# The dt step of a float32r decoder layer: its products cut at other column widths, h_hi and h_lo in one tile

## The chip, the cores and the metric

The kernel runs on one core of a Trainium2 chip. The metric is the device time of one execution in microseconds, lower is better; it is given as the median of three runs. All times below are microseconds unless a unit stands beside them, and times of day in the trace count from the start of the profiled span.

## The reference

One inference step of a decoder layer with two SwiGLU feed-forward blocks and a mixer between them, for 256 prompt tokens and 8 sample tokens (264 columns in all), D_MODEL 2048. The mixer begins with one large product, and the last 16 columns of that product are the `dt` values:

```python
proj = h @ p['w_in']                      # (tokens, 2048) @ (2048, IN_COLS)
xl, gl, z, xbc, dt_raw = jnp.split(proj, [o1, o2, o3, o4], axis=-1)
...
dt = jax.nn.softplus(dt_raw.astype(jnp.float32) + p['ssd_dt_bias'].astype(jnp.float32))
A = -jnp.exp(p['ssd_A_log'].astype(jnp.float32))
y, ssm_hT = ssd_scan(xs4, dt, A, ...)     # the state space scan uses dt as step width
```

The change concerns how `h @ w_in` is made for the `dt` columns, nothing else.

## The kernel before

Activations are held transposed: features on the 128 partitions, the 264 tokens (256 of the prompt, `NT`, and 8 samples, `NB`; together `COLS`) in the free dimension. A weight matrix is therefore the stationary operand, 128 x 128 at a time, and the activations stream past it, 264 columns a product, into a PSUM bank of 512 columns.

Every product is made three times in float32r: the weight w is split into `w_hi` (rounded to float32r) and `w_lo` (the rest), the activation h into `h_hi` and `h_lo`, and the product is w_hi h_hi + w_hi h_lo + w_lo h_hi. All three add up in the same PSUM columns.

The weights come in 90 steps of 8 pieces. For each piece SyncE issues the transfer into `raw` (four slots, two pieces in each; the slot is filled again when VectorE has split both pieces of the step before), ACT rounds it into `w_hi` (line 686, after the transfer and after TensorE has used the piece four places before it), VectorE makes `w_lo` = raw - w_hi (line 1007), and TensorE multiplies (lines 1660 to 1662, in `piece`). ACT and VectorE run up to four pieces ahead of TensorE. In each quarter j of a step ACT's and VectorE's queues hold first the splitting of pieces 2j+3 and 2j+4 (with j = 3 that is pieces 1 and 2 of the next step), then what else the step asks of them.

The steps around the change:

- step 38, xbc 0: a full step, 8 pieces of 4 x 256 weight columns, two 128-column halves each; 192 products.
- step 39, dt (`S_DT`): 8 pieces of 2 x 128 weight columns, one half; 48 products of 264 columns into bank 0 of `main`. At its end ACT copies `main[:, 0, 0:264]` to `dtq` in SBUF (line 824) and counts up `drained[0]`; it stands in ACT's queue behind the rounding of pieces 1 and 2 of step 40.
- step 40, xbc 1: a full step again. Its first pieces go to banks 0 and 1, so its first product waits until `drained[0]` shows that the dt result is copied. In VectorE's queue stand, in this order: w_lo of pieces 1 and 2 of step 40, the convolution of xbc 0 (`conv_taps(1)`, line 1214 on), w_lo of pieces 3 and 4.
- step 41, xbc 2: after its first pieces TensorE turns `dtq` round (line 1570 and 1574), and VectorE goes on with the softplus.

PSUM bank 1 of `main` (`main[:, 1, :]`) is not used by the dt step of the kernel before.

Of the kernel before, what the change touches and what calls it, by code (L numbers as in the profile page):

```python
# [22 lines left out]
F32R = mybir.dt.float32r  # L23
ALU = mybir.AluOpType
# [119 lines left out]
def build(nc, ins, outs):  # L144
    with ExitStack() as ctx:
# [5 lines left out]


        x = sb("x", [P, KD, COLS])
        h_hi = sb("h_hi", [P, KD, COLS], F32R)
        h_lo = sb("h_lo", [P, KD, COLS], F32R)
        raw = sb("raw", [P, 4, 2 * PIECE])
        w_hi = sb("w_hi", [P, 4, PIECE], F32R)
        w_lo = sb("w_lo", [P, 4, PIECE], F32R)
# [104 lines left out]
        aff_ready, hhi_ready, h_ready = sem("aff_ready"), sem("hhi_ready"), sem("h_ready")  # L263
        act_chain, dve_chain, pool_chain = sem("act_chain"), sem("dve_chain"), sem("pool_chain")

        dt_turned, cs_spread, dt_exp, dA_ready = sem("dt_turned"), sem("cs_spread"), sem("dt_exp"), sem("dA_ready")
        abs_ready, decl_sub, decl_ready, dexp_ready = sem("abs_ready"), sem("decl_sub"), sem("decl_ready"), sem("dexp_ready")
        samp_spread, samp_placed = sem("samp_spread"), sem("samp_placed")
# [730 lines left out]
        def _(dve):  # L999
# [298 lines left out]
            def dve_tasks(kind, t, j, s, o_, e_):  # L1298
                u = 4 * t + j
                if kind == "dt" and j == 3:  # L1300
                    conv_taps(1)
                if kind == "xbc":
                    if j in (1, 3) and u != 3:
# [261 lines left out]
        def _(pe):  # L1565
# [97 lines left out]
                last.then_inc(piece_used, 1)  # L1663


            def rows_batch(b):
                bank = (b5, b6)[b % 2]
                if b >= 2:
                    pe.wait_ge(rows_placed, b - 1)
                if b == 0:  # L1670
                    pe.wait_ge(consts_ready, 1)
                    pe.wait_ge(c_rows, C_ROWS)
                    for tile in range(C_TILES):
                        last = turn(bank[:, tile * P:(tile + 1) * P], rowbuf[:, tile, :])
                elif b == 1:
                    pe.wait_ge(early_rows, EARLY_ROWS)
                    for tile in range(C_TILES, E_TILES):
                        last = turn(bank[:, (tile - C_TILES) * P:(tile - C_TILES + 1) * P], rowbuf[:, tile, :])
                elif b < 2 + KD // 2:
                    pe.wait_ge(x_rows, 32)  # L1680
                    k = 2 * (b - 2)
                    for kk in range(2):
                        for c in range(2):
                            last = turn(bank[:, kk * NT + c * P:kk * NT + (c + 1) * P],
                                        xrows[:, c, (k + kk) * P:(k + kk + 1) * P])
                else:
                    pe.wait_ge(late_rows, LATE_ROWS)
                    pe.wait_ge(std_ready, 1)
                    at = E_TILES + 4 * (b - 2 - KD // 2)
                    for n, tile in enumerate(range(at, min(at + 4, ROW_TILES))):  # L1690
                        rows = min(P, ROWS - tile * P)
                        last = (turn if rows == P else turn_part)(
                            bank[:, n * P:n * P + rows], latebuf[0:rows, tile - E_TILES, :], *([rows] if rows < P else []))
                    if b == 3 + KD // 2:
                        last = MM(bank[:, 448:448 + 3 * NHEAD], ones[0:1, :], heads_row[0:1, :], start=True, stop=True)
                last.then_inc(rows_turned, 1)
# [131 lines left out]
            def pe_tasks(kind, t, j, e_):  # L1828
                u = 4 * t + j
                if kind == "xbc":  # L1830
                    if u == 4:
                        pe.wait_ge(drained[0], E_DT + 1)
                        pe.wait_ge(std_ready, 2)
                        turn(b6[:, 0:P], dtq[:, 0:P])
                        turn(b6[:, P:2 * P], dtq[:, P:2 * P])
                        turn_part(b6[0:NB, 2 * P:3 * P], dtq[:, 2 * P:2 * P + NB]).then_inc(dt_turned, 1)
                    if u == 7:
                        pe.wait_ge(dA_ready, 1)
                        both = dA[:, 0:2, :].rearrange("p c h -> p (c h)")
                        MM(b7[:, 0:32], tri[:, :], both, start=True, stop=True)  # L1840
                        MM(b7[:, 32:64], ones[:, :], both, start=True, stop=True).then_inc(cs_spread, 1)
                    if u == 10:
                        pe.wait_ge(dexp_ready, 1)
                        MM(b6[:, 0:2 * P].rearrange("p (a n) -> p a n", a=2), ones[0:NB, :],
                           sumsq[0:NB, :, 0:P], start=True, stop=True).then_inc(samp_spread, 1)
                if kind in ("lru", "z"):
                    r = u + (16 if kind == "z" else 0)
                    if r == 0:
                        prep(0)
                    if r == 2:  # L1850
                        states_turned()
                    if r == 3:
                        states(0)
                    if 5 <= r <= 12:
                        y_item(r - 5)
                    if 16 <= r <= 23:
                        y_item(r - 8)
                    if 4 <= r <= 11:
                        bcast(r - 4)
                    if r == 13:  # L1860
                        prep(1)
                    if r == 14:
                        states(1)
                    if 15 <= r <= 22:
                        bcast(r - 7)
                if kind == "lru":
                    if j < 2:
                        col_rows(2 * t + j)
                    else:
                        gates(2 * t + j - 2)  # L1870
                if kind == "out" and u == 1:
                    pe.wait_ge(captured, 10)
                    pe.wait_ge(h_captured, 4)
                    for tile in range(OUT_TILES):
                        bank = (b5, b6)[tile // 4]
                        if tile == 4:
                            pe.wait_ge(std_ready, 3)
                        last = turn(bank[:, (tile % 4) * P:(tile % 4 + 1) * P], outcol[:, tile * P:(tile + 1) * P])
                        if tile == 3 or tile == OUT_TILES - 1:
                            last.then_inc(out_turned, 1)  # L1880
                if kind == "out" and u == 15:
                    pe.wait_ge(out_rows_ready, 1)
                    sums_and_products(4, S_FF2)
# [14 lines left out]
            for n, seg in enumerate(plan):  # L1898
# [11 lines left out]
                for i, last in turns(seg):  # L1910
                    for k in range(per):
                        s, e_, o_, par = at_step(seg, i, k)
                        for j in range(4):
                            if j == 0 and s not in GAP_STEPS:
                                for a in products_at.get(s, ()):
                                    ada_product(a)
                            for m in (2 * j, 2 * j + 1):
                                if s == S_OUT and m == 2:
                                    pe.wait_ge(y_placed, 16)
                                    sumsq_total(3)  # L1920
                                if pk == "full":
                                    par_m, at = full_place(s, m)
                                else:
                                    par_m, at = par, sum(PIECES[pk][:m])
                                piece(s, m, pk, par_m, at, None if pk == "full" and par_m else h_base,
                                      act_base, (e_, o_)[par_m] if at == 0 else None, kind == "down")
                            if j == 2 and s in vec_ends:
                                ada_turn(vec_ends[s])
                            if kind not in ("up", "down"):
                                pe_tasks(kind, what or 0, j, e_)  # L1930
                            if j == 2 and S_LAST <= s < S_LAST + 4:
                                g = s - S_LAST
                                pe.wait_ge(mod_ready, SHF + 3)
                                if g:
                                    pe.wait_ge(shift_copied, g)
                                for q in range(4):
                                    last_mm = MM(b5[:, q * P:(q + 1) * P], mods[:, SHF, 4 * g + q, 0:1].to_broadcast([P, P]),
                                                 ident[:, :], start=True, stop=True)
                                last_mm.then_inc(shift_made, 1)
# [65 lines left out]
```

## Time and profile before

| | us |
|---|---|
| median of three runs | 2169.36 |
| lowest and highest of the runs | 2167.39, 2170.27 |
| span of the profiled execution, first to last instruction | 2166.7 |
| TensorE busy with matmuls in it | 2116.9 (98%) |
| VectorE busy | 1210.2 (56%) |
| ACT busy | 860.4 (40%) |

The own time of the profiled execution is not listed beside its span; the median of the runs lies 2.7 us above that span. In the trace a matmul's row gives its start and a modelled duration; matmuls are pipelined, so the time that one costs is read from start to start. A product in plain fp32 leaves two MATMUL records, one in float32r leaves one. The granted clock is given as a share of 2.4 GHz.

### The profile page before, as it was taken

Reading aid. Unit: us, or ns where it says so; the run is one execution under the profiler, and the core shown is the slowest. Engines: PE = TensorE matmul, PEld = TensorE weight load, DVE = VectorE, ACT = ScalarE, POOL = GpSimd, SP = SyncE. Lnnn points to the kernel's source line nnn. Section 1 sums busy time; section 2 is a strip of 40 time slices with the busy share of each in tenths; the row PEclk is TensorE's granted clock in tenths of the full one; section 3 lists DMA queues with packets and bytes.
Section 4 is the critical chain, followed back from the end, with each engine's and each line's share of the span. In section 5 each row is a group of like instructions: output and inputs, shape, how many; then the busy total and the mean of one; then the engine's idle time right before and its main releaser. Section 6 shows DMA issues by size and latency. Waiting matters only on the chain.

```text
span 2166.7 us, 40038 instructions
## 1 busy us (share of the span) xinstructions
PE 2116.9 (98%) x17437; PEld 1977.3 (91%) x17437; DVE 1210.2 (56%) x1649; ACT 860.4 (40%) x1058; POOL 123.2 (6%) x148
## 2 busy tenths in 40 slices
PE   6999999999999999989999999999999999999998
PEld 4989889988888889989988998999998999999998
DVE  4356676434444445577789967444444444445555
ACT  3433343333333333356665534333333333333332
POOL 0000000000000000011774000000000000000000
PEclk8999999999999999999999999999999999999999
DMA  9998877799888877756555486774667877655453
GB/s 356 345 305 307 294 277 270 251 366 349 310 312 306 309 271 250 244 157 203 161 175 163 153 278 218 249 246 164 242 230 256 303 272 245 241 174 166 147 177 117
DMA packets 394269, 534.17 MB, mean 247 GB/s; under 512 B 13031, under 2 KB 357999, under 8 KB 375407
## 3 DMA queue, kind: packets, MB, share of 16 engines
q1 hardware_dynamic: 371792, 519.28, 70.1%
q10 hardware_dynamic: 22303, 12.33, 2.0%
q8 instruction: 138, 2.26, 0.4%
q14 instruction: 36, 0.29, 0.0%
HBM read 524.37 MB, written 7.19 MB: 245 GB/s over the span
## 4 chain that ended last, share of the span: by engine, by line
PE 92%; DVE 5%; DMA 1%; ACT 1%; issue 1%; SPq 1%; ACTq 0%; DVEq 0%
PE main L1660 24%; PE main L1661 24%; PE main L1662 23%; PE b L1583 5%; PE main L1726 4%; PE main L1728 4%; PE main L1727 4%; PE b L1593 1%; DVE w_lo L1007 1%; PE b L1606 1%; DMA first<-in_w_ada 1%; DVE ntile L1105 1%; SPq L530 1%; DVE h_lo L1110 1%; PE b L1777 0%
## 5 line engine op out<-in xcount | busy, mean ns | idle before, releaser
L1007 DVE TENSOR_TENSOR w_lo<-raw,w_hi 128x1024 fp32r<-128x1024 f32 (+2 forms) x720 | 792.1, 1107 | 806.3 <-ACT w_hi L686 804.7
L686 ACT ACTIVATE w_hi<-raw 128x1024 fp32r<-128x1024 f32 (+2 forms) x720 | 685.8, 956 | 1076.1 <-PE main L1662 908.6
L1660 PE MATMUL main<-h_hi,w_hi 128*128 128x264 f32 x2960 | 851.3, 288 | 11.8 <-DVE h_lo L1118 3.9
L1661 PE MATMUL main<-h_lo,w_hi 128*128 128x264 f32 x2960 | 843.6, 285 | 0.0
L1662 PE MATMUL main<-h_hi,w_lo 128*128 128x264 f32 x2960 | 842.2, 285 | 0.0
L1660 PEld LDWEIGHTS main<-h_hi,w_hi 128*128 128x128 f32 x2960 | 559.2, 189 | 32.0 <-DVE w_lo L1007 20.7
L1661 PEld LDWEIGHTS main<-h_lo,w_hi 128*128 128x128 f32 x2960 | 557.9, 188 | 0.4
L1662 PEld LDWEIGHTS main<-h_hi,w_lo 128*128 128x128 f32 x2960 | 557.6, 188 | 0.0
L1660 PE MATMUL main<-act_hi,w_hi 128*128 128x264 f32 x1408 | 402.1, 286 | 0.0
L1662 PE MATMUL main<-act_hi,w_lo 128*128 128x264 f32 x1408 | 400.4, 284 | 0.0
L1661 PE MATMUL main<-act_lo,w_hi 128*128 128x264 f32 x1408 | 399.8, 284 | 0.0
L1660 PEld LDWEIGHTS main<-act_hi,w_hi 128*128 128x128 f32 x1408 | 264.6, 188 | 10.1 <-issue 9.2
L1661 PEld LDWEIGHTS main<-act_lo,w_hi 128*128 128x128 f32 x1408 | 265.3, 188 | 0.0
L1662 PEld LDWEIGHTS main<-act_hi,w_lo 128*128 128x128 f32 x1408 | 264.6, 188 | 0.0
L1726 PE MATMUL main<-h_hi,w_hi 128*128 128x264 f32 x704 | 203.8, 290 | 4.6 <-DVE h_lo L1074 4.3
L1728 PE MATMUL main<-h_hi,w_lo 128*128 128x264 f32 x704 | 200.7, 285 | 0.0
L1727 PE MATMUL main<-h_lo,w_hi 128*128 128x264 f32 x704 | 200.5, 285 | 0.0
L1726 PEld LDWEIGHTS main<-h_hi,w_hi 128*128 128x128 f32 x704 | 133.6, 190 | 16.0 <-issue 11.5
L1727 PEld LDWEIGHTS main<-h_lo,w_hi 128*128 128x128 f32 x704 | 133.8, 190 | 0.0
L1728 PEld LDWEIGHTS main<-h_hi,w_lo 128*128 128x128 f32 x704 | 133.3, 189 | 0.0
L1583 PE MATMUL b<-ada,cT 128*32 128x512 f32 x1024 | 116.9, 595 | 0.0
L1583 PEld LDWEIGHTS b<-ada,cT 128*32 128x32 f32 x1024 | 29.8, 109 | 61.9 <-issue 57.0
(278 smaller groups left out, 1006.9 us busy)
## 6 DMA issues: line engine op xcount, KB each, us to landing
raw<-in_w_up SPq DMA_DIRECT2D x132, 1024.0 KB, 5.2
ada<-in_w_ada SPq DMA_DIRECT2D x112, 1024.0 KB, 8.6
raw<-in_w_down SPq DMA_DIRECT2D x96, 768.0 KB, 5.3
raw<-in_w_up SPq DMA_DIRECT2D x88, 512.0 KB, 5.1
raw<-in_w_in SPq DMA_DIRECT2D x36, 1024.0 KB, 5.4
ada<-in_w_ada_f SPq DMA_DIRECT2D x32, 1024.0 KB, 10.1
ada<-in_w_ada SPq DMA_DIRECT2D x56, 512.0 KB, 7.6
raw<-in_w_down SPq DMA_DIRECT2D x32, 512.0 KB, 4.4
```

Of the source, the lines that this page charges most:

```text
L530: sp.dma_start(quarter_slot(i)[:, v], quarter_columns(0, i, v)).then_inc((ada_landed, first_landed)[i // 4][i % 4], 16)
L686: A(split_view(w_hi, m, kind), raw_piece(m, kind), ACT.Copy).then_inc(hi_done, 1)
L1007: TT(split_view(w_lo, m, kind), raw_piece(m, kind), split_view(w_hi, m, kind).bitcast(F32), ALU.subtract).then_inc(lo_done, 1)
L1105: STT(ntile[:, k % 4, :], x[:, k, 0:NT], gain[:, k, 0:1], rstd[:, 0:NT], ALU.mult, ALU.mult).then_inc(aff_ready, 1)
L1110: return STT(h_lo[:, k, 0:NT], ntile[:, k % 4, :], mods[:, shift, k, 0:1], h_hi[:, k, 0:NT].bitcast(F32), ALU.add, ALU.subtract)
L1583: last = MM(b4[32 * j:32 * j + 32, :], cT[:, k, :], ada[:, k % 4, j * 512:(j + 1) * 512], start=k == 0, stop=k == KD - 1, tile_position=(0 ...
L1660: MM(out, wh, hi[:, k, :], start=k == 0, stop=False)
L1661: MM(out, wh, lo[:, k, :], start=False, stop=False)
L1662: last = MM(out, wl, hi[:, k, :], start=False, stop=k == total - 1)
L1726: MM(out, wh, h_hi[:, k, :], start=kk == 0, stop=False)
L1727: MM(out, wh, h_lo[:, k, :], start=False, stop=False)
L1728: last = MM(out, wl, h_hi[:, k, :], start=False, stop=kk == 3)
```

## The change

It changes the widths of the dt step's products, by groups of four k-rows (two pieces each):

- k 0 to 3 (pieces 0, 1): as before, 264 columns.
- k 4 to 7 (pieces 2, 3): 256 and 8 columns apart, so six products a k-row.
- k 8 to 11 (pieces 4, 5): the prompt's columns of h_hi and h_lo are one product of 512 columns with w_hi into bank 1, the two halves side by side; one product of 264 columns with w_lo, and two of 8 columns for the samples, go to bank 0.
- k 12 to 15 (pieces 6, 7): 128 and 136 columns apart, six products a k-row.

VectorE then adds the two halves of bank 1 to `dtq`, in two instructions, after ACT's copy and ahead of the convolution, and counts up a new semaphore `dt_added`. The first product of step 40 waits for it, as do the transposes of `dtq` in place of `drained[0]`. `h_hi` and `h_lo` become two halves of one tile, so that one access pattern can reach both.

```diff
-        h_hi = sb("h_hi", [P, KD, COLS], F32R)
-        h_lo = sb("h_lo", [P, KD, COLS], F32R)
+        h_both = sb("h_both", [P, 2, KD, COLS], F32R)
+        h_hi, h_lo = h_both[:, 0, :, :], h_both[:, 1, :, :]
...
+        dt_added = sem("dt_added")
...
                 if kind == "dt" and j == 3:
+                    dve.wait_ge(drained[0], e_ + 1)
+                    ch.link(TT(dtq[:, 0:NT], dtq[:, 0:NT], main[:, 1, 0:NT], ALU.add))
+                    TT(dtq[:, 0:NT], dtq[:, 0:NT], main[:, 1, NT:2 * NT], ALU.add).then_inc(dt_added, 1)
                     conv_taps(1)
...
+            def dt_piece(s, m, before=None):
+
+                pe.wait_ge(lo_done, s * 8 + (m + 1))
+                if before:
+                    pe.wait_ge(drained[0], before)
+                for kk in range(2):
+                    k = 2 * m + kk
+                    wh, wl = (w[:, m % 4, kk * P:(kk + 1) * P] for w in (w_hi, w_lo))
+                    groups = {0: [slice(0, COLS)], 1: [slice(0, NT), slice(NT, COLS)],
+                              2: [], 3: [slice(0, P), slice(P, COLS)]}[m // 2]
+                    for c in groups:
+                        out = main[:, 0, c]
+                        MM(out, wh, h_hi[:, k, c], start=k == 0, stop=False)
+                        MM(out, wh, h_lo[:, k, c], start=False, stop=False)
+                        last = MM(out, wl, h_hi[:, k, c], start=False, stop=k == KD - 1 and c is groups[-1])
+                    if not groups:
+                        MM(main[:, 1, :], wh, h_both[:, :, k, 0:NT], start=k == 8, stop=k == 11)
+                        MM(main[:, 0, 0:COLS], wl, h_hi[:, k, :], start=False, stop=False)
+                        MM(main[:, 0, NT:COLS], wh, h_hi[:, k, NT:COLS], start=False, stop=False)
+                        last = MM(main[:, 0, NT:COLS], wh, h_lo[:, k, NT:COLS], start=False, stop=False)
+                last.then_inc(piece_used, 1)
...
                     if u == 4:
-                        pe.wait_ge(drained[0], E_DT + 1)
+                        pe.wait_ge(dt_added, 1)
...
                             for m in (2 * j, 2 * j + 1):
+                                if kind == "dt":
+                                    dt_piece(s, m, e_ if m == 0 else None)
+                                    continue
...
+                                if s == S_DT + 1 and m == 0:
+                                    pe.wait_ge(dt_added, 1)
                                 piece(s, m, pk, par_m, at, None if pk == "full" and par_m else h_base,
                                       act_base, (e_, o_)[par_m] if at == 0 else None, kind == "down")
```

## Rows read from the trace of the kernel before

**Rows 1.** The page: TensorE's busy time and share, and the chain by engine.

```profile
PE 2116.9 (98%) x17437; PEld 1977.3 (91%) x17437; DVE 1210.2 (56%) x1649; ACT 860.4 (40%) x1058; POOL 123.2 (6%) x148
PE 92%; DVE 5%; DMA 1%; ACT 1%; issue 1%; SPq 1%; ACTq 0%; DVEq 0%
```

**Rows 2.** Busy time by stretch: dt's products, the hole, step 40; columns in first row.

```profile
core 0: us, PE busy (x) PEld busy (x) DVE busy (x) ACT busy (x) POOL busy (x), PEclk, DMA share, GB/s
966.20:972.18 5.98, 5.98 (x50) 5.77 (x48) 3.12 (x6) 4.10 (x7) 0.00 (x0) 1.00 0.88 282
972.18:974.29 2.11, 0.00 (x1) 0.03 (x1) 1.76 (x3) 1.48 (x3) 0.00 (x0) 1.00 1.07 352
974.29:997.00 22.71, 21.54 (x173) 20.94 (x173) 16.96 (x47) 15.45 (x22) 2.22 (x12) 1.00 0.78 217
```

**Rows 3.** Timeline, TensorE: start, duration, names, shapes, idle before; first, last, next.

```profile
966.20 0.28 PE L1660 MATMUL main<-h_hi,w_hi 128*128 128x264 f32 x1
...
971.90 0.28 PE L1662 MATMUL main<-h_hi,w_lo 128*128 128x264 f32 x1
974.29 0.36 PE L1660 MATMUL main<-h_hi,w_hi 128*128 128x264 f32 x1 [2.11 <-ACT part L824]
```

**Rows 4.** Timeline, ACT: roundings of weights, the copy of dt.

```profile
969.38 0.42 ACT L686 ACTIVATE w_hi<-raw 128x256 fp32r<-128x256 f32 x1 [0.31 <-PE main L1662]
970.10 2.01 ACT L686 ACTIVATE w_hi<-raw 128x1024 fp32r<-128x1024 f32 x2 [0.31 <-PE main L1662]
972.82 1.06 ACT L686 ACTIVATE w_hi<-raw 128x1024 fp32r<-128x1024 f32 x1 [0.70 <-DMA raw<-in_w_in]
973.78 0.37 ACT L824 ACTIVATE part<-main 128x264 f32<-128x264 f32 x1
...
978.20 2.01 ACT L686 ACTIVATE w_hi<-raw 128x1024 fp32r<-128x1024 f32 x2 [2.29 <-PE main L1662]
```

**Rows 5.** Timeline, VectorE: the rests of the weights, the convolution.

```profile
969.83 0.42 DVE L1007 TENSOR_TENSOR w_lo<-raw,w_hi 128x256 fp32r<-128x256 f32 x1 [0.30 <-ACT w_hi L686]
...
973.90 1.22 DVE L1007 TENSOR_TENSOR w_lo<-raw,w_hi 128x1024 fp32r<-128x1024 f32 x1 [0.35 <-ACT w_hi L686]
975.49 1.83 DVE L1214 SCALAR_TENSOR_TENSOR cfull<-cin,small,cfull 128x288 f32<-128x288 f32 x4 [0.37 <-ACT cfull L769]
```

**Rows 6.** The chain that ended last, in order of time, one link.

```profile
967.36 5.43 DMA raw<-in_w_in
```

**Rows 7.** Timeline, TensorE, near the end: fp32 products of 1 and 8 columns.

```profile
2154.96 1.05 PE L1965 MATMUL b<-ones,sumsq 128*128 128x1 f32 x8 [1.56 <-DVE part L1147]
2155.88 0.59 PE L1967 MATMUL b<-sumsq,ones 128*128 128x8 f32 x4
2156.32 0.41 PE L1570 MATMUL main<-ident,x 128*128 128x128 f32 x2
```

**Rows 8.** Timeline, TensorE: fp32 products of 128 columns, two records each.

```profile
1071.14 0.39 PE L1777 MATMUL b<-tri,dA 128*128 128x128 f32 x2
1071.37 0.39 PE L1780 MATMUL b<-later,ident 128*128 128x128 f32 x2
1071.59 0.50 PE L1810 MATMUL b<-ident,xbc 128*128 128x128 f32 x3
```

**Rows 9.** Timeline, TensorE: two fp32 products of 512 columns, four records, and what follows.

```profile
1045.48 1.88 PE L1761 MATMUL b<-xdec,btok 128*128 128x512 f32 x4
1047.20 0.61 PE L1825 MATMUL b<-cval,gates_w 128*128 128x264 f32 x2
```

**Rows 10.** Groups by line and shape, VectorE: busy us, mean ns, idle before.

```profile
L1255 DVE TENSOR_TENSOR cbm<-b,tri 128x256 f32<-128x256 f32 x2 | 0.8, 416 | 0.0
```

**Rows 11.** Timeline, TensorE: the first product after a hole of 2.29 us.

```profile
1082.22 1.22 PE L1825 MATMUL b<-cval,gates_w 128*128 128x264 f32 x2 [2.29 <-issue]
```

**Rows 12.** Busy time by stretch around 1082; columns as in rows 2.

```profile
1081.00:1081.50 0.50, 0.00 (x0) 0.00 (x0) 0.50 (x1) 0.00 (x0) 0.50 (x1) 1.00 0.00 0
1082.00:1082.50 0.50, 0.28 (x1) 0.31 (x2) 0.50 (x2) 0.00 (x0) 0.50 (x2) 0.50 0.00 0
1084.50:1085.00 0.50, 0.50 (x5) 0.50 (x3) 0.50 (x1) 0.50 (x2) 0.00 (x0) 0.50 0.00 0
1085.50:1086.00 0.50, 0.50 (x6) 0.50 (x6) 0.50 (x3) 0.50 (x1) 0.00 (x0) 1.00 0.62 92
```

## The prediction, written before the changed kernel ran

> **What bounds the kernel now.** The page comes first. TensorE's matmuls are busy for 98% of the span and hold 92% of the chain that ended last [rows 1], so nearly every microsecond that TensorE gains or loses shows in the end time. The change touches one of the 90 weight steps, the dt step (step 39), so the next view is the table by stretch around it [rows 2]: 5.98 us of products without a hole, then 2.11 us in which TensorE does nothing, then the next step (step 40, the second xbc step). The granted clock is 1.00 in all three, the 2.4 GHz level. The rows of TensorE itself [rows 3] give the price of one product: the 48th starts at 971.90, the first at 966.20, so 5.70 / 47 = 0.121 us from start to start, each with a weight load of its own. Step 40 starts at 974.29, released by ACT's copy of the dt result.
>
> Why there is a hole stands in ACT's and VectorE's rows [rows 4, 5] and in one link of the chain [rows 6]. Between the dt step's products and that copy ACT has to round one more weight piece of step 40 (piece 2, start 972.82), and that piece waits for a weight transfer that takes 5.43 us from 967.36. The copy follows at 973.78 and ends at 974.15; TensorE starts 0.14 later. VectorE's own share of piece 2 (w_lo, 973.90, 1.22 us) was nobody's concern so far: it ends at 975.12, after TensorE has begun. So the hole is a second limit that lies beside the products: if the products end later, the first 1.5 us or so of that are free; whatever VectorE does before step 40 was free too, and no longer is.
>
> **The products, part by part.** The 16 k-rows become four groups of four. Before, a k-row is three products of 264 columns, 0.363 us. A price for narrower float32r products is not in this trace: all have 264 columns. The nearest rows:
> - 8 columns: the products of 8 and of 1 columns near the end, each with a 128-column weight load as here [rows 7]. Four records of 8 columns take 2156.32 - 2155.88 = 0.44 us, 0.11 each; eight of 1 column take 0.92, 0.115 each. A product can't come faster than its weight load, it seems, whatever its width. These are plain fp32, where one product is two records; a float32r product is one. I take 0.11; below it the price by columns (0.121 x 8/264 = 0.004), above it two such records, 0.22.
> - 128 and 136 columns: by the same floor 0.11. By columns 0.06; as a full fp32 product of 128 columns 0.22 to 0.23 [rows 8], and 0.234 for 136. I take 0.11, since a float32r product is one record like those of rows 7 and its weight load is the same 128 x 128.
> - 256 columns: next to the 264 ones, 0.12 (by columns 0.118).
> - 512 columns: the fp32 products of 512 columns pass the columns twice per record, four records in 1047.20 - 1045.48 = 1.72 us [rows 9], 0.43 each, so 0.215 for one pass.
>
> Group 0 (pieces 0, 1) is unchanged: 12 x 0.121 = 1.45 us. Group 1: three products of 256 and three of 8 per row: 12 x (0.12 + 0.11) = 2.76. Group 2: one of 512, one of 264, two of 8 per row: 4 x (0.215 + 0.121 + 0.22) = 2.22. Group 3: six per row: 24 x 0.11 = 2.64. Together 9.07 us against 48 x 0.121 = 5.82: **3.25 us more of TensorE**. With a last product of about 0.27 us the step ends at 966.20 + 9.07 - 0.11 + 0.27 = 975.43 in place of 972.18.
>
> **The added wait.** The two halves of group 2 land in two more stretches of a second bank, and VectorE adds them to the copy, one after the other (the second waits for the first through a semaphore). Step 40's first product now waits for the second addition; every later product is queued behind it on TensorE. The additions stand in VectorE's queue behind w_lo of pieces 1 and 2 of step 40, and the convolution of rows 5 (975.49) and w_lo of pieces 3, 4 stand behind them. Price of one: 0.416 us for the same shape out of PSUM [rows 10], plus some 0.03 of hand-over (ACT's w_hi of 969.38 ends at 969.80, VectorE starts at 969.83): 2 x 0.45 = 0.9 us. A float32 256-column w_lo at 0.42 [rows 5] says the same.
>
> Now what is late: piece 6 of dt ends at 975.43 - 1.32 = 974.11, so ACT rounds piece 2 of step 40 from 974.21 (the 0.1 us is that of 970.10 behind dt's piece 4, whose last product ends 970.00) instead of 972.82; the transfer has landed by then. VectorE follows 1.08 later, as in the rows before: 975.29 to 976.51. ACT copies the dt result at 975.53 to 975.90, so it is w_lo that is last. Additions 976.51 to 977.4, TensorE at about **977.5, 3.2 us later than 974.29**. Of the 3.25 us of products the old hole hides most, and w_lo and the additions open a hole of the same size again.
>
> Is it given back later? ACT's splits for step 40 are 1.4 to 1.8 us late, TensorE 3.2, so weights are earlier with respect to TensorE than before; piece 3 of it was ready at about 978.20 + 2.3 = 980.5 [rows 4] (the 1.08 and 1.22 of above), 2.5 us ahead of its use at 974.29 + 3 x 2.9 = 983.0, and gains 1.4 us on it. TensorE is busy 21.54 of the 22.71 us of step 40 [rows 2], and after it the chain is TensorE's products again. So the shift stays whole. Moving h_hi and h_lo into one tile changes no stride and no place of note: zero, and no gain is excluded by a row, only by the absence of any access that differs. The other new wait (the transposes in step 40's successor) waits for an event long past: zero.
>
> The profiled execution has a span of 2166.7 us, and the median of the runs is 2169.36, 2.7 us around it. 2166.7 + 3.2 = 2169.9 of span; with the same 2.7 around it, **2172.6 us**.
>
> **Rivals.** One, *narrow products at the price of full fp32*. If float32r keeps its one pass only from some width on, 128 and 136 columns cost 0.22 and 0.234, group 3 costs 12 x 0.454 = 5.45, the dt step 11.88 us and ends at 978.13. w_lo is then in time, and the path is copy (0.1 + 0.37), additions (0.9), start (0.1): 979.6, **+5.3 us**. If 8 columns also cost 0.22, groups 1 and 2 cost 4.08 and 3.10, the step 14.1 us: **+7.5**. It decides from 0.19 us per product of group 3 on: there the shift passes 4.3 us, which is 0.2% of the time. For it: rows 8 are the only 128-column products with such operands that aren't transposes. Against it: one record per product, where full fp32 has two.
>
> Two, *the price goes by columns*, the weight loads being hidden. Then the dt step stays at about 5.8 us, piece 2 waits for its transfer as before, w_lo ends at 975.12, additions 976.0, TensorE 976.1: **+1.8 us**. Rows 7 speak against it. The Trainium skill, TensorE: Matmul & The Clock Gate, section Back-to-back issue gap, has for warm products the columns over 2.4 GHz plus 2.5 ns, and about 25 ns for the smallest; by that page an estimate of the dt step is 5.9 us, which gives this rival's time. The trace does not agree for loads of 128 columns: 0.11 us for 8 columns.
>
> Three, *the clock falls in the hole*. The trace has a hole of 2.29 us [rows 11] in which the granted clock went from 1.00 to 0.50, and back some 3.5 us later [rows 12]; 3 us of products at half speed lose 1.5. The hole at 972.18 had 2.11 us and no fall. The new one is 977.5 - 975.4 = 2.1 us. A fall makes it 3.2 + 1.5 = **+4.7 us**. The same two-sided luck holds for the hole of rows 11, which the shift moves: up to 1.5 us either way.
>
> **How the numbers follow.** 0.2% of this time (4.3 us) is about what a measurement here can tell from no change. Forecast (+3.2, clock holds) 0.46; rival three 0.13; rival one 0.29; rival two 0.08; anything else 0.04. Slower by over 0.2%: nearly all of rival one (0.28), most of three (0.09), a tenth of the forecast through the later hole (0.05): 0.43 with a rest. Faster would need a gain of 4.3 us, for which no row offers a source: 0.02. The remainder, 0.55, is within. The range goes from 2170.0 (rival two at 2171.2 and a fall less elsewhere) to 2177.0 (the dear end of rival one).
>
> **What would show it.** Right: records of 8, 128 and 136 columns start every 0.11 us, the 512 ones take 0.21 to 0.22, the step's products last 9.1 us, the first product of step 40 is released by VectorE's second addition some 2 us after the last dt product, at about 977.5. Rival one: twice the spacing in group 3, or two records per product. Rival two: a dt step near 5.8 us. Wrong altogether: step 40 starting before 976, or TensorE waiting for weights in step 40.

## The result and the profile after

The changed kernel takes 2171.76 us in the median (20 runs, 2170.75 to 2173.87), the kernel before 2168.98 (20 runs, 2167.39 to 2172.05). The ratio is 1.0014 with a 95% interval of 1.0008 to 1.0020: 2.8 us slower, between 1.7 and 4.3. That is within 0.2%, and 0.4 us from the forecast of 3.2 us. The forecast time of 2172.6 us lies 0.8 us above the measured median: it was built on the median of three runs of the kernel before, 2169.36, where that of twenty is 2168.98.

The page of the changed kernel, as in [rows 1]: TensorE's busy time and share.

```profile
PE 2121.8 (98%) x17465; PEld 1983.5 (91%) x17465; DVE 1212.8 (56%) x1651; ACT 861.1 (40%) x1058; POOL 125.7 (6%) x148
```

Busy time by stretch, as in [rows 2]: the dt step's products, the hole behind them, the first part of step 40. The column after the engines is the granted clock.

```profile
965.19:974.53 9.34, 9.34 (x78) 9.02 (x76) 4.67 (x8) 5.26 (x8) 0.00 (x0) 1.00 0.93 300
974.53:976.44 1.91, 0.00 (x1) 0.00 (x1) 1.88 (x4) 1.84 (x5) 0.62 (x4) 1.00 1.10 354
976.44:979.98 3.54, 3.54 (x17) 3.54 (x17) 2.96 (x9) 1.34 (x2) 0.38 (x2) 0.53 1.11 342
```

The products last 9.34 us to the end of the last one, where they lasted 5.98; the hole is 1.91 us where it was 2.11. And behind it the clock is at half, which it was not in the profile of the kernel before.

The timeline of TensorE, as in [rows 3]: a k-row of group 1, a k-row of group 2, the end of group 3, the start of step 40.

```profile
966.65 0.28 PE L1682 MATMUL main<-h_both,w_hi 128*128 128x256 f32 x1
...
967.00 0.17 PE L1682 MATMUL main<-h_both,w_hi 128*128 128x8 f32 x1
967.03 0.25 PE L1683 MATMUL main<-h_both,w_hi 128*128 128x8 f32 x1
967.14 0.25 PE L1684 MATMUL main<-h_both,w_lo 128*128 128x8 f32 x1
967.26 0.37 PE L1682 MATMUL main<-h_both,w_hi 128*128 128x256 f32 x1
...
969.33 0.48 PE L1686 MATMUL main<-h_both,w_hi 128*128 128x512 f32 x1
969.64 0.28 PE L1687 MATMUL main<-h_both,w_lo 128*128 128x264 f32 x1
969.77 0.17 PE L1688 MATMUL main<-h_both,w_hi 128*128 128x8 f32 x1
969.80 0.25 PE L1689 MATMUL main<-h_both,w_hi 128*128 128x8 f32 x1
969.91 0.48 PE L1686 MATMUL main<-h_both,w_hi 128*128 128x512 f32 x1
...
971.65 0.31 PE L1682 MATMUL main<-h_both,w_hi 128*128 128x128 f32 x1
...
974.25 0.28 PE L1684 MATMUL main<-h_both,w_lo 128*128 128x136 f32 x1
976.44 0.44 PE L1664 MATMUL main<-h_both,w_hi 128*128 128x264 f32 x1 [1.91 <-DVE part L1304]
976.68 0.42 PE L1665 MATMUL main<-h_both,w_hi 128*128 128x264 f32 x1
976.90 0.42 PE L1666 MATMUL main<-h_both,w_lo 128*128 128x264 f32 x1
```

One record per product, in every width. A k-row of group 1 takes (969.33 - 966.65) / 4 = 0.67 us, one of group 2 (971.65 - 969.33) / 4 = 0.58. In group 3 the 24th product starts 2.60 us after the first, 2.60 / 23 = 0.113 each. In step 40 the products start every 0.22 us in place of 0.121: that is the half clock.

The single starts are uneven: 0.03 us after the first product of 8 columns, 0.31 after one of 512. The weight loads (PEld, same columns) are not. From group 1 the loads for three products of 8 columns and for the product of 256 behind them, then two loads of group 2, between which the product of 512 columns runs:

```profile
966.89 0.19 PEld L1682 LDWEIGHTS main<-h_both,w_hi 128*128 128x128 f32 x1
967.01 0.19 PEld L1683 LDWEIGHTS main<-h_both,w_hi 128*128 128x128 f32 x1
967.12 0.19 PEld L1684 LDWEIGHTS main<-h_both,w_lo 128*128 128x128 f32 x1
967.23 0.19 PEld L1682 LDWEIGHTS main<-h_both,w_hi 128*128 128x128 f32 x1
...
969.41 0.19 PEld L1687 LDWEIGHTS main<-h_both,w_lo 128*128 128x128 f32 x1
969.65 0.19 PEld L1688 LDWEIGHTS main<-h_both,w_hi 128*128 128x128 f32 x1
```

Loads start 0.11 to 0.12 us apart around the products of 8 columns, and 0.24 apart where a product of 512 lies between.

ACT and VectorE between the dt step and step 40, as in [rows 4, 5]: the rounding of piece 2 and the copy; then w_lo of piece 2 and the two additions.

```profile
973.28 1.06 ACT L687 ACTIVATE w_hi<-raw 128x1024 fp32r<-128x1024 f32 x1 [0.34 <-PE main L1684]
974.57 0.39 ACT L825 ACTIVATE part<-main 128x264 f32<-128x264 f32 x1 [0.22 <-PE main L1684]
```

```profile
974.38 1.23 DVE L1008 TENSOR_TENSOR w_lo<-raw,w_hi 128x1024 fp32r<-128x1024 f32 x1 [0.17 <-ACT w_hi L687]
975.52 0.41 DVE L1303 TENSOR_TENSOR part<-part,main 128x256 f32<-128x256 f32 x1
975.97 0.42 DVE L1304 TENSOR_TENSOR part<-part,main 128x256 f32<-128x256 f32 x1
```

Piece 2's rounding is now released by TensorE (the piece of the dt step that holds its place), not by a transfer. The copy ends at 974.96, w_lo at 975.61, and the additions follow w_lo at once: w_lo is what they wait for.

### The profile page after: what moved, and what is told of

It is laid out like the page before. It is cut to its first block, busy times and chain, and to the rows that moved or that the text cites. A ratio compares the mean times of both kernels' runs of the same rounds, so it can differ in the third digit from the quotient of the medians.

```text
span 2170.5 us, 40096 instructions
## 1 busy us (share of the span) xinstructions
PE 2121.8 (98%) x17465; PEld 1983.5 (91%) x17465; DVE 1212.8 (56%) x1651; ACT 861.1 (40%) x1058; POOL 125.7 (6%) x148
## 4 chain that ended last, share of the span: by engine, by line
PE 89%; DVE 6%; ACT 1%; DMA 1%; SPq 1%; issue 1%; POOL 0%; ACTq 0%; DVEq 0%; POOLq 0%
PE main L1664 23%; PE main L1665 23%; PE main L1666 23%; PE b L1587 5%; PE main L1752 4%; PE main L1754 4%; PE main L1753 4%; DVE w_lo L1008 2%; PE b L1597 1%; SPq L531 1%; PE b L1610 1%; DVE ntile L1106 1%; DMA first<-in_w_ada 1%; ACT w_hi L687 1%; DVE h_both L1111 1%
## 5 line engine op out<-in xcount | busy, mean ns | idle before, releaser
L1664 PE MATMUL main<-h_both,w_hi 128*128 128x264 f32 x2944 | 848.5, 288 | 10.7 <-DVE h_both L1119 3.9
L1665 PE MATMUL main<-h_both,w_hi 128*128 128x264 f32 x2944 | 841.2, 286 | 0.0
L1666 PE MATMUL main<-h_both,w_lo 128*128 128x264 f32 x2944 | 839.9, 285 | 0.0
L1664 PEld LDWEIGHTS main<-h_both,w_hi 128*128 128x128 f32 x2944 | 558.5, 190 | 30.5 <-DVE w_lo L1008 18.4
L1665 PEld LDWEIGHTS main<-h_both,w_hi 128*128 128x128 f32 x2944 | 557.1, 189 | 0.4
L1666 PEld LDWEIGHTS main<-h_both,w_lo 128*128 128x128 f32 x2944 | 556.8, 189 | 0.0
L1752 PE MATMUL main<-h_both,w_hi 128*128 128x264 f32 x704 | 203.6, 289 | 4.1 <-DVE h_both L1075 3.8
L1754 PE MATMUL main<-h_both,w_lo 128*128 128x264 f32 x704 | 200.4, 285 | 0.0
L1753 PE MATMUL main<-h_both,w_hi 128*128 128x264 f32 x704 | 200.2, 284 | 0.0
L1752 PEld LDWEIGHTS main<-h_both,w_hi 128*128 128x128 f32 x704 | 133.3, 189 | 15.5 <-issue 11.5
L1753 PEld LDWEIGHTS main<-h_both,w_hi 128*128 128x128 f32 x704 | 133.6, 190 | 0.0
L1754 PEld LDWEIGHTS main<-h_both,w_lo 128*128 128x128 f32 x704 | 133.0, 189 | 0.0
```

The lines of the kernel that those rows point to most:

```text
L1664: MM(out, wh, hi[:, k, :], start=k == 0, stop=False)
L1665: MM(out, wh, lo[:, k, :], start=False, stop=False)
L1666: last = MM(out, wl, hi[:, k, :], start=False, stop=k == total - 1)
L1752: MM(out, wh, h_hi[:, k, :], start=kk == 0, stop=False)
L1753: MM(out, wh, h_lo[:, k, :], start=False, stop=False)
L1754: last = MM(out, wl, h_hi[:, k, :], start=False, stop=kk == 3)
```

## The experiments

The measure that is most exact in a profile is the time from the dt step's first product to step 40's first product. In the kernel before it is 974.29 - 966.20 = 8.09 us, in the changed one 976.44 - 965.19 = 11.25.

| kernel | dt step's first start to last end | hole | step 40 after the dt step's start | clock in step 40 | ratio of times, interval |
|---|---|---|---|---|---|
| before, first profile | 5.98 | 2.11 | 8.09 | full | 1 |
| before, second profile (e8) | 5.98 | 1.95 | 7.93 | half, after 0.8 us | one time: 2168.77 us |
| one tile (e7) | 5.98 | 2.04 | 8.02 | half, after 1.5 us | 1.0006, 0.9997 to 1.0015 |
| changed | 9.34 | 1.91 | 11.25 | half at first | 1.0014, 1.0008 to 1.0020 |
| changed, second profile (e9) | 9.34 | 1.91 | 11.25 | half, after 1.5 us | one time: 2172.53 us |
| narrow groups alone (e1) | 8.48 | 0.57 | 9.05 | full | 1.0002, 0.9993 to 1.0011 |
| second bank alone (e2) | 6.85 | 5.06 | 11.91 | half at first | 1.0007, 0.9998 to 1.0016 |
| before, copy first (e3) | 5.98 | 0.57 | 6.56 | full | 0.9988, 0.9979 to 0.9997 |
| changed, copy first (e4) | 9.34 | 1.39 | 10.73 | full | 1.0004, 0.9995 to 1.0013 |
| finer cuts (e5) | 19.31 | 0.57 | 19.88 | half at first | one time: 2180.78 us |
| finer cuts, 32 weight columns (e6) | 6.16 | 4.38 | 10.54 | half at first | one time: 2172.89 us |

### The widths alone (e1)

```diff
-                              2: [], 3: [slice(0, P), slice(P, COLS)]}[m // 2]
+                              2: [slice(0, COLS)], 3: [slice(0, P), slice(P, COLS)]}[m // 2]
```

with the additions and the waits for `dt_added` taken out.

> The widths alone: groups 1 and 3 (256 and 8, 128 and 136 columns) as in the change, group 2 back at 264 columns, no second bank, no additions, no added wait. Theory (weight loads set the price of a narrow product, 0.11 us each, and the old hole hides most of it): the dt step lasts 1.45 + 2.76 + 1.45 + 2.7 = 8.4 us of starts, its last product ends 8.5 us after its first starts; then only ACT's copy stands before step 40 (0.05 + 0.39 + 0.14), so step 40 starts 9.1 us after the dt step instead of 8.09: +1.0 us, a hole of 0.6 us. Rival a (products are not hidden by the hole): +2.6 us. Rival b (only the added wait costs): 0 us.

Measured: 2169.51 us against 2169.11 (1.0002). Step 40's first product in its timeline:

```profile
974.41 0.36 PE L1660 MATMUL main<-h_both,w_hi 128*128 128x264 f32 x1 [0.57 <-ACT part L824]
```

The hole of 0.57 us and the released-by-ACT are as the theory has them: step 40 comes 9.05 us after the dt step, where 9.1 was expected, and 0.96 later than in the first profile before, from 2.5 us more of products. So the old hole covers most of the narrow products' cost, as long as nothing else is put behind them; rival a falls. Rival b is told apart only by this row, not by the time, whose interval (1.5 us less to 2.4 more) holds both.

### The second bank alone (e2)

```diff
-                    groups = {0: [slice(0, COLS)], 1: [slice(0, NT), slice(NT, COLS)],
-                              2: [], 3: [slice(0, P), slice(P, COLS)]}[m // 2]
+                    groups = [] if m // 2 == 2 else [slice(0, COLS)]
```

> The second bank alone: group 2 as in the change (512, 264, 8, 8 columns), with the two additions and the added wait; groups 0, 1 and 3 at 264 columns. Theory (w_lo of step 40's piece 2 and the two additions are the last to come, and piece 2 waits for its transfer): the dt step lasts 3 x 1.45 + 4 x 0.58 = 6.7 us, its last product ends 6.85 us after its first starts; piece 2 is rounded 6.6 us after that start as before, w_lo ends at 8.9, the additions at 9.8, step 40 starts at 9.9 instead of 8.09: +1.8 us, with a hole of 3 us; if the granted clock falls in that hole, 1.6 us more, +3.4. Rival a (only longer products cost): +0.9 us. Rival b (the additions are hidden): 0 to +0.5 us.

Measured: 2171.23 us against 2169.11 (1.0007), in the timed runs 2.1 us more (0.4 less to 3.5 more). The dt step is 6.85 us long as expected, but the hole of this profile is 5.06 us, 2 us beyond the theory. The chain shows why (start, duration, what):

```profile
966.72 7.58 DMA raw<-in_w_in
...
974.32 1.06 ACT w_hi L687
...
975.41 1.23 DVE w_lo L1008
976.63 0.34 DVE part L1303
977.00 0.43 DVE part L1304
```

The order is the one foreseen: transfer, rounding, w_lo, two additions. But the transfer took 7.58 us here and 5.43 in [rows 6]. The order stands, the size of one of its terms varies. The profiled execution was the slowest of the eleven, 2172.85 us, so its hole need not be that of the others. By this chain rivals a and b both fall: the step's own products end only 0.9 us later, and the additions are in the chain. The time's interval holds them both.

### The copy ahead of the rounding that waits (e3 and e4)

In both ACT copies the dt result after rounding piece 1 of step 40 and before piece 2; in e4 VectorE also makes the two additions before w_lo of piece 2.

```diff
-                            pieces_ahead(s, j, PIECE_KIND[kind], follows)
+                            if kind == "dt" and j == 3:
+                                hi_piece(s + 1, 1, follows)
+                                act.wait_ge(piece_used, 8 * S_DT + 8)
+                                A(dtq, main[:, 0, 0:COLS], ACT.Copy).then_inc(drained[0], 1)
+                                hi_piece(s + 1, 2, follows)
+                            else:
+                                pieces_ahead(s, j, PIECE_KIND[kind], follows)
```

This is ACT's part; not shown are the copy's old place, which goes, and in e4 the like for VectorE.

> The kernel before with one thing moved: ACT copies the dt result after rounding piece 1 of step 40 and before rounding piece 2, which waits for a transfer. Theory (the hole of 2.11 us before step 40 is that order): the copy follows the last dt product by 0.05 us, takes 0.37, step 40 starts 0.14 later, 6.55 us after the dt step's start instead of 8.09; weights of pieces 0 to 2 are ready before their use: -1.5 us. Rival (the next limit, weights of step 40, stands right behind): 0 us.

> The changed kernel with ACT's copy of the dt result ahead of the rounding of step 40's piece 2, and VectorE's two additions ahead of w_lo of that piece. Theory (of the new hole of 1.91 us w_lo is the part that the additions wait for): after the last dt product copy 0.05 + 0.39, additions 0.03 + 0.86, start 0.06: a hole of 1.4 us, step 40 starts 10.8 us after the dt step instead of 11.25: 0.45 us less than the changed kernel, +2.7 us against the kernel before. Rival (the additions and the copy themselves are the hole): no difference to the changed kernel, +3.2 us.

Measured, e3: 2166.04 us against 2169.11, ratio 0.9988 (0.9979 to 0.9997): 3.1 us faster than the kernel before, between 0.7 and 4.6. In its timelines step 40's first product and the copy:

```profile
971.03 0.36 PE L1664 MATMUL main<-h_hi,w_hi 128*128 128x264 f32 x1 [0.57 <-ACT part L975]
```

```profile
970.50 0.39 ACT L975 ACTIVATE part<-main 128x264 f32<-128x264 f32 x1
970.97 1.06 ACT L686 ACTIVATE w_hi<-raw 128x1024 fp32r<-128x1024 f32 x1
```

The hole shrinks from 2.11 to 0.57 us and step 40 comes 6.56 us after the dt step, 1.53 sooner, where the theory had 6.55. The timed gain is twice that, though its interval holds 1.5; what the rest may be stands below (the clock).

Measured, e4: 2169.63 against 2169.11 (1.0004). VectorE's additions and step 40's first product:

```profile
974.48 0.42 DVE L1532 TENSOR_TENSOR part<-part,main 128x256 f32<-128x256 f32 x1 [0.78 <-ACT part L976]
974.94 0.42 DVE L1533 TENSOR_TENSOR part<-part,main 128x256 f32<-128x256 f32 x1
```

```profile
975.41 0.39 PE L1672 MATMUL main<-h_both,w_hi 128*128 128x264 f32 x1 [1.39 <-DVE part L1533]
```

The hole is 1.39 us, the theory's 1.4: the additions, 0.93 us from the first's start to step 40, are the longest part of it, the copy the rest. w_lo was worth 0.5 us of the changed kernel's hole; the rival falls by this row. In the time e4 is 2 us better than forecast; its interval, 1.1 us less to 2.8 more, holds the forecast, and the clock, below, may account for half of it.

### What a narrow product costs (e5 and e6)

Both cut the dt step finer: groups 0 to 3 at 264, 132, 88 and 66 columns, all into the first bank, no additions. e6 loads only 32 of the 128 weight columns of each product.

```diff
+                    n_cut = (1, 2, 3, 4)[m // 2]
+                    each = COLS // n_cut
+                    groups = [slice(i * each, (i + 1) * each) for i in range(n_cut)]
...
-                    wh, wl = (w[:, m % 4, kk * P:(kk + 1) * P] for w in (w_hi, w_lo))
+                    wh, wl = (w[:, m % 4, kk * P + 96:(kk + 1) * P] for w in (w_hi, w_lo))
...
-                        out = main[:, 0, c]
+                        out = main[0:32, 0, c]
```

(the last two changes are e6's alone; there VectorE reads the dt values at the place that goes with the 32 columns).

> The dt step's products cut finer and finer, all with 128-column weight loads and into the first bank, no additions: group 0 at 264 columns, group 1 at 132 (two), group 2 at 88 (three), group 3 at 66 (four). Theory (a product narrower than its weight load costs the weight load, some 0.113 us, whatever its width): 12 x 0.121 + 24 x 0.113 + 36 x 0.113 + 48 x 0.113 = 13.7 us from start to start, and step 40 starts 14.4 us after the dt step, 6.3 us later than in the kernel before. Rival a (price by columns plus a few ns): a dt step of 6 to 6.5 us, 0 us. Rival b (four passes below some width): 0.22, 0.15 and 0.11 us in groups 1, 2 and 3, 17.4 us.

> The same cuts of 264, 132, 88 and 66 columns, but only the 32 of the 128 weight columns in which the dt values lie are loaded and multiplied; the other 96 hold values of other columns that nothing uses. Theory (the weight load sets the price of narrow products): loads of 32 columns are four times shorter, so the products go by columns: about 0.113, 0.058, 0.04 and 0.03 us, 5.6 us of dt step; step 40 then waits for its transfer as in the kernel before, 0 us. Rival (a fixed gap from product to product, whatever is loaded): 0.113 us in all of groups 1 to 3 as in the run with full loads, 13.7 us and +6.3 us.

Measured, e5: 2180.78 us beside 2168.28, one time. Its timeline, the starts of groups 1 and 2 and where the spacing changes:

```profile
966.65 0.22 PE L1679 MATMUL main<-h_both,w_hi 128*128 128x132 f32 x1
...
969.27 0.25 PE L1679 MATMUL main<-h_both,w_hi 128*128 128x88 f32 x1
...
972.26 0.31 PE L1679 MATMUL main<-h_both,w_hi 128*128 128x88 f32 x1
972.37 0.42 PE L1680 MATMUL main<-h_both,w_hi 128*128 128x88 f32 x1
972.58 0.42 PE L1681 MATMUL main<-h_both,w_lo 128*128 128x88 f32 x1
...
974.07 0.40 PE L1679 MATMUL main<-h_both,w_hi 128*128 128x66 f32 x1
...
984.10 0.40 PE L1681 MATMUL main<-h_both,w_lo 128*128 128x66 f32 x1
```

24 products of 132 columns in 2.62 us, 0.109 each; the first 27 of 88 columns in 2.99, 0.111 each. Then 0.21 each, whatever the width. The stretches of this kernel say what happened at 972.3:

```profile
969.30:972.30 3.00, 3.00 (x30) 3.00 (x28) 0.43 (x1) 1.19 (x2) 0.00 (x0) 1.00 1.07 368
974.28:984.50 10.22, 10.22 (x48) 10.08 (x48) 2.45 (x2) 2.11 (x2) 0.00 (x0) 0.50 0.58 187
```

The granted clock fell to 0.50 while TensorE ran without a pause. So the price holds as the theory says (0.109 and 0.111 us, not 0.22 or 0.15, and not by columns), and the total was missed by 5.5 us (step 40 19.9 us after the dt step, not 14.4), since the theory had no clock in it.

Measured, e6: 2172.89 us, one time. Its timeline:

```profile
968.21 0.22 PE L1679 MATMUL main<-h_both,w_hi 128*32 128x132 f32 x1
...
969.68 0.20 PE L1679 MATMUL main<-h_both,w_hi 128*32 128x88 f32 x1
...
971.16 0.19 PE L1679 MATMUL main<-h_both,w_hi 128*32 128x66 f32 x1
...
972.72 0.19 PE L1681 MATMUL main<-h_both,w_lo 128*32 128x66 f32 x1
```

With loads of a quarter of the columns, 24 products of 132 columns take 1.47 us, 0.061 each, and 36 of 88 columns 1.48, 0.041 each; 47 spacings of 66 columns take 1.56, 0.033 each. What differs from e5 is the number of weight columns (and with it of the result's partitions), so full loads are what a narrow product pays for. That it is the load itself is said by the loads' own records, 0.19 us each in e5 and 0.11 in e6, and by those of the changed kernel, which start every 0.11 us around products of 8 columns. The rival falls. Step 40 came 2.5 us later than in the first profile before, not 0: a transfer of 7.88 us in its chain made a hole of 4.38.

The Trainium skill, TensorE: Matmul & The Clock Gate, section LDWEIGHTS, has the load in ns as columns over 1.2, by which an estimate for 128 columns is 107 ns: the 0.109 us at full clock agrees. The Trainium skill, on the same page, section Back-to-back issue gap, gives the second rival's rule for an isolated product and says that at small widths it under-counts, the load not being in it: the rule agrees with e6 (an estimate of 55 + 2.5 = 58 ns at 132 columns, 61 measured) and not with e5.

### One tile alone, and second profiles (e7, e8, e9)

e7 has only the four lines of the change that make h_hi and h_lo halves of `h_both`; e8 and e9 are the kernel before and the changed one, as they are.

> The kernel before with h_hi and h_lo as halves of one tile and nothing else. Theory: no difference, 0 us in the time and 0.121 us per product. Rival (two streams from one tile meet somewhere): the products of all steps slow down, some us in all. The hole before step 40 is also read again: theory (the copy waits for the rounding of piece 2, and that for its transfer) says that step 40 starts some 1.5 us after that transfer lands, whether it took 5.4 us as in the profile of the kernel before or 7.6 as in that of the second bank alone.

> The kernel before, profiled a second time. Theory (the hole before step 40 is as long as the transfer of piece 2 makes it): step 40 starts 1.5 us after that transfer lands; with a transfer of 7 us or more the hole is 3.5 us or more, and the change, whose longer products cover such a transfer, then costs that much less than against the first profile. Rival (the transfer takes 5.4 us always, and 7.6 us was the doing of the second bank): the hole is 2.1 us again.

> The changed kernel, profiled a second time. Theory (the products and the added wait cost the same in each execution, the granted clock does not): the dt step again lasts 9.2 us from start to start, the hole is 1.9 us and step 40 starts 11.2 to 11.3 us after the dt step; the clock falls to half behind the hole in some executions, as it did in two of three profiles without the change, and then costs 1.3 to 1.6 us in step 40. Rival (the narrow products bring the fall about in the changed kernel each time): a fall again, and the change then costs that much more than the hole and the products. One more look can only refute the rival (no fall) or leave both standing.

Measured, e7: 2169.67 us against 2168.28, 1.0006 with an interval that holds 1; the dt step's 48 products again take 5.98 us. No cost is seen, and up to 0.15% is not excluded.

e8, the kernel before once more: the transfer took 5.27 us, e7's took 5.36, and the holes are 1.95 and 2.04: step 40 some 1.5 us after the landing, as the theory says, with the short transfer each time. So the long transfer was in none of the three profiles of the old order; why it took 7.6 and 7.9 us in e2 and e6 stays open. What e8 shows besides is in the stretch at the start of step 40 (first row); the second is e9's, the changed kernel again:

```profile
973.19:976.50 3.31, 3.31 (x18) 3.31 (x19) 2.94 (x6) 1.58 (x4) 0.82 (x4) 0.63 1.10 349
...
978.43:981.80 3.37, 3.37 (x18) 3.37 (x17) 2.40 (x6) 1.51 (x2) 0.38 (x2) 0.50 1.21 280
```

The clock falls behind the old hole too, in this profile and in e7's, where the first profile shows none. e9 repeats the changed kernel: hole 1.91, step 40 11.25 us after the dt step, and a fall 1.5 us into step 40. The first 40 spacings of step 40 take 4.98 us in the first profile before, 6.48 in e8, 6.44 in e7 and 6.51 in both profiles of the changed kernel. So a fall costs about 1.5 us, in two of three profiles of the old order and in both of the changed kernel. Taking the mean of the profiles, from the first product of step 38 to the end of the span: 1227.3, 1228.5 and 1228.8 without the change (1228.2), 1232.1 and 1231.9 with it (1232.0). That is 3.8 us, inside the timed interval of 1.7 to 4.3.

The clock also accounts for much of e3 and e4. From the same point e3 ends at 1225.8, 2.4 us below that mean: 1.5 of hole, and 0.9 that fits a fall (1.5 us) that two profiles in three have and e3, with its hole of 0.57 us, has not. e4 ends at 1229.9, 1.7 above the mean and not 2.7 above. Whether the narrow products of groups 1 and 3 bring the fall nearer in the changed kernel isn't settled: two profiles with a fall are what the rival expects, and also what the hole alone may give. e1 and e4 have the narrow products, smaller holes and no fall; e5 has a fall among narrow products without any hole.

## Why the prediction was right

**The price of the narrow products** was the step with the widest bounds. 0.11 us for 8, 128 and 136 columns, taken from [rows 7], measured 0.113 in group 3; group 1 2.68 us for 2.76 foreseen, group 2 2.32 for 2.22 (512 columns took 0.24 from load to load, not 0.215), group 3 2.71 (2.60 and one spacing) for 2.64, group 0 1.46 for 1.45. The sum is 9.17 us for 9.07. The price shows in whole k-rows and in the loads, not in each product's start as the prediction's signs had it. e5, e6 and the loads show the reason that the prediction only supposed.

**The hole.** ACT's rounding of piece 2 released by TensorE, w_lo the last to come, then two additions, then step 40: all in that order in the rows after. 11.25 us from the dt step to step 40 for 11.3 foreseen, so +3.2 as forecast against 8.09, 7.93 and 8.02. The hole of 1.91 us was 2.1 in the sum, since in the rows w_lo's end and the first addition overlap by 0.09 us where the sum put them end to end; and the products ended 0.11 us later than foreseen, while the rounding of piece 2 began only 0.08 later.

**What was mis-sized** is the third rival. The forecast was "+3.2, clock holds", and the clock did not hold: both profiles of the changed kernel show the fall, to which the prediction gave a chance of 0.13, and at the price of 1.5 us that it named. It did not give the old hole a fall, on a single profile that has none; two of three of the old order have one. The error cancels for the most part, because it stands on both sides: +3.2 from the hole and the products, some 0.5 from the clock (1.5 against two thirds of 1.5), 3.8 in the mean of the profiles; the timed difference is 2.8. So the products and the added wait were right by their mechanism, and that the total came so near is in part luck. The 1.0 us between 3.8 and 2.8 is within the interval; the two profiled executions of the changed kernel, at 2172.29 and 2172.53 us, were 0.5 and 0.8 above its median, which is a part of it, and the rest stays open. Luck is in the absolute time too: the prediction put 2.7 us between span and time, where each run since has 1.7 to 1.9, so its profiled execution was some 0.9 us faster than the median it was set beside.

**Rival one** (narrow products at the price of full fp32) and **rival two** (price by columns) are out: one record per product and 0.11 us, in e5 down to 88 columns at full clock. Rival two is true only where the load is short (e6). **The shift is not given back**: the 3.8 us in the mean of the profiles still stand at the end of the span, as the prediction held. It could have been, at a place that the prediction passed over. The 21.54 us of work in 22.71 of [rows 2] leave out a hole of 1.17 us ahead of step 40's last piece, where TensorE waits for VectorE. First the kernel before, then the changed one:

```profile
996.95 0.39 PE L1660 MATMUL main<-h_hi,w_hi 128*128 128x264 f32 x1 [1.17 <-DVE w_lo L1007]
...
1000.61 0.39 PE L1664 MATMUL main<-h_both,w_hi 128*128 128x264 f32 x1 [1.17 <-DVE w_lo L1008]
```

The hole is as long as before, so VectorE came later by as much as TensorE. The products that turn `dtq` round, on whose result VectorE's softplus hangs, stand in step 40 after its first two pieces (980.26 in the kernel before), not in step 41. The hole of [rows 11], for which the prediction allowed 1.5 us either way, changes nothing either: it reads 2.29 us in the first profile and 1.05 to 1.07 in e7, e8, e9 and the first of the changed kernel, but from its start to the end of the span all five take 1086.7 to 1086.9 us.

**One tile** costs nothing that can be seen, as forecast.

**A version that beats both** came out of the same reading: the hole in the kernel before was an order in ACT's queue, the copy behind a rounding that waits for a transfer. With the copy one place earlier (e3) the kernel takes 2166.04 us, 0.12% below the kernel before and 5.7 us below the median of the changed one, those two in different comparisons.

## What to carry to other kernels

A stretch in which the main engine stands still is cover, but for one thing only: price what is put into it from the rows of who ends it, and look at what else its releaser has queued ahead. A product narrower than its weight load costs the load, so cutting it saves nothing, and loading fewer weight columns shortens it (e6's products show that; its one time, with the long transfer in it, shows no gain). One profile shows one throw of the clock: a hole of some 2 us needs a second profile before its fall, or its absence, is taken for the kernel's own.

## What the runs showed of the hardware that was not expected

- The granted clock can fall with TensorE never idle: in e5 from 1.00 to 0.50 at 972.3, after 5.6 us of products of 132 and 88 columns behind loads of 128, and it stayed at half over the 10.2 us of the 66-column products.
- At half clock the weight load takes twice as long as well: 47 spacings of 66-column products in 10.03 us, 0.213 each, where the load-bound price at full clock is 0.109 to 0.111.
- A float32r product of 264 columns costs 0.121 us with a load of 32 columns too (e6's group 0: 12 in 968.21 - 966.75 = 1.46 us), so that price is the columns' own and not the load's.
- The same transfer of the weights of step 40 took 5.27 to 5.43 us in three profiles and 7.58 and 7.88 in two others; the cause is open.
